# A two-layer hybrid transformer on one core: the end of the first layer's mixer, its second norm and its first feed-forward tiles, done by halves of the token columns

## What is computed

```
def modulate(x, g, shift, scale):
    return rms_norm(x, g) * (1 + scale) + shift
...
        acc = gates[..., 0, :] * (outs[0] @ w_branch[0])
...
        return acc @ w_out
...
def sq_relu_mlp(h, w1, w2):
    return jnp.square(jax.nn.relu(h @ w1)) @ w2
...
        x = x + g1 * o_lat
        x = x + g2 * sq_relu_mlp(modulate(x, norm2_g[l], sh2, sc2), w_ff1[l], w_ff2[l])
        if need_ctx:
            x_ctx = x_ctx + cg1 * o_ctx
            x_ctx = x_ctx + cg2 * sq_relu_mlp(modulate(x_ctx, norm2_g[l], csh2, csc2), w_ff1[l], w_ff2[l])
```

## Time and profile before

| | us |
|---|---|
| median of 3 runs | 1434.37 |
| the three runs | 1432.66, 1434.37, 1436.02 |
| the profiled execution | 1435.79 |
| its span in the trace | 1434.0 |
| PE busy in it | 1403.9 (98%) |
| DVE, ACT, POOL busy | 950.1 (66%), 656.4 (46%), 209.4 (15%) |
| mean granted clock of PE | 0.998 |

### The profile page before, as it was taken

The page is one execution under the profiler, slowest core; times in us unless marked ns, Lnnn a source line. Parts: engine busy times, 40 slices in busy tenths (PEclk is TensorE's granted clock), DMA queues, the critical chain, the costliest instruction groups (busy, mean ns, idle before and its releaser), DMA issues.

```text
span 1434.0 us, 24978 instructions
## 1 busy us (share of the span) xinstructions
PE 1403.9 (98%) x10474; PEld 1217.8 (85%) x10474; DVE 950.1 (66%) x1479; ACT 656.4 (46%) x969; POOL 209.4 (15%) x172
## 2 busy tenths in 40 slices
PE   8999999999999999999999999999999999999999
PEld 4889877786678888888888888889888779999999
DVE  6797467857446666699756655588387955775564
ACT  5722534364164444543224423553365645564462
POOL 0000001334111220131002200000013511121130
PEclk9999999999999999999999999999999999999999
DMA  9632323033153323266555665141343334556553
GB/s 383 233 110 75 112 101 133 30 100 110 42 193 128 130 84 146 97 217 247 199 204 190 211 217 177 49 142 61 106 153 129 125 126 148 176 206 206 191 194 116
DMA packets 37409, 215.07 MB, mean 150 GB/s; under 512 B 4017, under 2 KB 7729, under 8 KB 13617
## 3 DMA queue, kind: packets, MB, share of 16 engines
q1 hardware_dynamic: 37298, 213.48, 42.3%
HBM read 211.37 MB, written 2.10 MB: 149 GB/s over the span
## 4 chain that ended last, share of the span: by engine, by line
PE 87%; DVE 6%; ACT 3%; DMA 1%; issue 1%; POOL 0%; SPq 0%; DVEq 0%; ACTq 0%
PE ps L1234 11%; PE ps L1235 11%; PE ps L1236 11%; PE ps L608 9%; PE ps L609 9%; PE ps L610 9%; PE ps L833 3%; PE ps L585 2%; PE ps L620 2%; PE ps L622 1%; PE ps L621 1%; DVE parts L2052 1%; DVE arena L2433 1%; PE ps L730 1%; PE ps L1177 1%
## 5 line engine op out<-in xcount | busy, mean ns | idle before, releaser
L1236 PE MATMUL ps<-parts 128*128 128x512 f32 (+1 forms) x960 | 314.0, 327 | 0.0
L610 PE MATMUL ps<-parts 128*128 128x512 f32 (+1 forms) x944 | 313.6, 332 | 0.0
L1234 PE MATMUL ps<-parts 128*128 128x512 f32 (+1 forms) x928 | 303.6, 327 | 0.0
L1235 PE MATMUL ps<-parts 128*128 128x512 f32 (+1 forms) x928 | 303.6, 327 | 0.0
L1602 ACT ACTIVATE parts<-ring 128x1024 fp32r<-128x1024 f32 x124 | 124.4, 1051 | 221.8 <-PE ps L1236 186.7
L2094 DVE TENSOR_TENSOR parts<-ring,parts 128x1024 fp32r<-128x1024 f32 x124 | 150.9, 1258 | 112.1 <-ACT parts L1602 111.9
L1236 PEld LDWEIGHTS ps<-parts 128*128 128x128 f32 x960 | 182.9, 191 | 12.9
L610 PEld LDWEIGHTS ps<-parts 128*128 128x128 f32 x944 | 180.2, 191 | 13.9
L1234 PEld LDWEIGHTS ps<-parts 128*128 128x128 f32 x928 | 176.8, 191 | 12.6 <-DVE parts L2102 0.2
L1235 PEld LDWEIGHTS ps<-parts 128*128 128x128 f32 x928 | 176.8, 191 | 12.4
L608 PE MATMUL ps<-parts 128*128 128x512 f32 (+1 forms) x544 | 185.2, 340 | 1.0 <-ACT arena L1855 1.0
(11 more groups left out here) (323 smaller groups left out, 2478.8 us busy)
## 6 DMA issues: line engine op xcount, KB each, us to landing
ring<-in_w_ff SPq DMA_DIRECT2D x64, 1024.0 KB, 4.8
ring<-in_w_in SPq DMA_DIRECT2D x58, 1024.0 KB, 4.9
ring<-in_w_mod_rows SPq DMA_DIRECT2D x31, 1024.0 KB, 4.8
arena<-in_w_mod SPq DMA_DIRECT2D x8, 1024.0 KB, 17.4
arena<-in_w_mod_rows SPq DMA_DIRECT2D x8, 1024.0 KB, 10.7
ring<-in_w_branch SPq DMA_DIRECT2D x32, 256.0 KB, 5.2
ring<-in_w_out SPq DMA_DIRECT2D x8, 1024.0 KB, 4.9
ring<-in_w_in SPq DMA_DIRECT2D x6, 512.0 KB, 12.1
```

Source lines behind the costliest of these rows:

```text
L610: last = pe.matmul(ps[0:m, 0:n], w_lo[:, k, c], hi, start=False, stop=(k == KD - 1))
L1234: pe.matmul(ps[:, 0:nt], w_hi[:, k, c], hi, start=(k == 0), stop=False)
L1235: pe.matmul(ps[:, 0:nt], w_hi[:, k, c], lo, start=False, stop=False)
L1236: last = pe.matmul(ps[:, 0:nt], w_lo[:, k, c], hi, start=False, stop=(k == kt - 1))
```

## The change

Three things are done for the latents (half 0) first and for the context (half 1) after, in the first layer only:

- output tiles 6 and 7: PE makes 6 and 7 for the latents, then 6 and 7 for the context, each by 24 matmuls of 256 columns (`last_output_tiles`). The squares' sum of the latents stands between the context's tile 6 and tile 7.
- the second norm: squares, sum, root, norm and split by halves on ACT and DVE (two new `norm_halves`). The sum of the context stands on PE inside the feed-forward, behind feature tile 2 of the latents.
- the first four feed-forward tiles: all eight feature tiles for the latents, then all eight for the context (`ff_first_halves`).

The five products of `busy` fall away in the first layer. ACT's copy of feed-forward block 1 now stands behind the square of tile 5 and ahead of that of tile 6; DVE's subtraction stands ahead of the sum of square 5 and of the residual of tile 6. SP's list is the same. The second layer keeps its code.

```diff
@@ -745,6 +757,59 @@
...
+            def last_output_tiles(l):
+                w_hi, w_lo = split(l, ("out", 3))
+                for s in range(2):
+                    a = slice(s * LAT, (s + 1) * LAT)
+                    for m in (KD - 2, KD - 1):
+                        key = ("wo", l, m) if s else ("wo", l, m, "first")
+                        ps = bank(key)[:, 0:LAT]
+                        c = slice((m % 2) * P, (m % 2 + 1) * P)
+                        if s and m == KD - 1:
+                            half_sum(l, 1, 0)
+                        for k in range(KD):
+                            if s == 0 and m == KD - 2 and k % 4 == 0:
+                                pe.wait_ge(*s_ml.at(("w", l, ("out", 3), k // 4)))
+                            hi, lo = [in_turns(x[:, k, a]) for x in (A_HI, A_LO)]
+                            pe.matmul(ps, w_hi[:, k, c], hi, start=(k == 0), stop=False)
+                            pe.matmul(ps, w_hi[:, k, c], lo, start=False, stop=False)
+                            last = pe.matmul(ps, w_lo[:, k, c], hi, start=False, stop=(k == KD - 1))
+                        last.then_inc(*product.up(key))
+                new_last[("out", l, 3)] = ("wo", l, KD - 1)
+            def half_sum(l, w, s):
+                ps = bank(("ss", l, w, s), fixed=s)
+                a = slice(s * LAT, (s + 1) * LAT)
+                pe.wait_ge(*s_sum.at(("sum", l, w, KD - 2, s)))
+                pe.matmul(ps[:, 0:LAT], tab("ones"), ACC[:, 0, a], start=True, stop=False)
+                pe.wait_ge(*s_sq.at(("sq", l, w, KD - 1, s)))
+                pe.matmul(ps[:, 0:LAT], tab("ones"), ACC[:, KD - 1, a], start=False, stop=True)\
+                    .then_inc(*product.up(("ss", l, w, s)))
+            def ff_first_halves(l):
+                tiles = [(f, j, bank(ff_product(l, f, j))) for f in range(2) for j in range(2)]
+                for s in range(2):
+                    a = slice(s * LAT, (s + 1) * LAT)
+                    for k in range(KD):
+                        pe.wait_ge(*s_h.at(("h", l, 1, k, s)))
+                        for f, j, ps in tiles:
+                            w_hi, w_lo = [w.rearrange("p (k c) -> p k c", k=KD)[:, k, j * P:(j + 1) * P] for w in ff_parts(l, f)]
+                            if s == 0 and j == 0 and k % 4 == 0:
+                                pe.wait_ge(*s_wlo.at((l, f, k // 4)))
+                            pe.matmul(ps[:, a], w_hi, in_turns(H_HI[:, k, a]), start=(k == 0), stop=False)
+                            pe.matmul(ps[:, a], w_lo, in_turns(H_HI[:, k, a]), start=False, stop=False)
+                        pe.wait_ge(*s_hl.at(("hl", l, k, s)))
+                        for f, j, ps in tiles:
+                            w_hi = ff_parts(l, f)[0].rearrange("p (k c) -> p k c", k=KD)[:, k, j * P:(j + 1) * P]
+                            last = pe.matmul(ps[:, a], w_hi, in_turns(H_LO[:, k, a]), start=False, stop=(k == KD - 1))
+                            if s and k == KD - 1:
+                                last.then_inc(*product.up(ff_product(l, f, j)))
+                        if s == 0 and k == 2:
+                            half_sum(l, 1, 1)
...
@@ -1326,13 +1391,17 @@
                     mla_output(l, t)
                 gate(l, MLA, AHEAD[l] - 1)
                 merge(l, MLA, ahead=[(MLA, m) for m in range(AHEAD[l])])
-                for b in range(4):
+                for b in range(4 if l else 3):
                     for j in range(2):
                         parted(("wo", l, 2 * b + j), l, ("out", b), j, A_HI[:, :, inner(l)], A_LO[:, :, inner(l)], nt,
                                "a" if b + j == 0 else None)
                     new_last[("out", l, b)] = ("wo", l, 2 * b + 1)
-                norm_sum(l, 1)
-                ff_first(l)
+                if l == 0:
+                    last_output_tiles(l)
+                    ff_first_halves(l)
+                else:
+                    norm_sum(l, 1)
+                    ff_first(l)
                 for f in range(1, FF_STEPS):
                     if f > 1:
...
+            def root(l, w, s):
+                a = slice(s * LAT, (s + 1) * LAT)
+                ps = read(act, ("ss", l, w, s))
+                freed(("ss", l, w, s), "squares", ("ln", l, w, s))
+                act.activation(RS[:, 0, a], ps[:, 0:LAT], ACT.Ln, bias=tab("eps")).then_inc(*s_sq.up(("ln", l, w, s)))
+                act.wait_ge(*s_sq.at(("ln", l, w, s)))
+                act.activation(RS[:, 0, a], RS[:, 0, a], ACT.Exp, scale=-0.5).then_inc(*s_sq.up(("rt", l, w, s)))
...
+            def norm_halves(l):
+                def half_square(k, s):
+                    a = slice(s * LAT, (s + 1) * LAT)
+                    act.wait_ge(*s_x.at(("x" if s else "first", l, 0, k)))
+                    act.activation(ACC[:, k, a], X[:, k, a], ACT.Square, scale=D ** -0.5).then_inc(*s_sq.up(("sq", l, 1, k, s)))
+                def half_high(k, s):
+                    a = slice(s * LAT, (s + 1) * LAT)
+                    act.wait_ge(*s_nrm.at(("n", l, 1, k, s)))
+                    act.activation(H_HI[:, k, a], NR[:, k, a], ACT.Identity, bias=modv[:, l, 24 + k, s:s + 1])\
+                        .then_inc(*s_h.up(("h", l, 1, k, s)))
+                act.preload_act_table_set("natural_log_exp_and_others")
+                for k in range(KD - 2):
+                    if k in (0, 2, 4):
+                        part_high(l, ("out", 1 + k // 2))
+                    square(l, 1, k)
+                    if k in (4, 5):
+                        split_high(l, k - 4)
+                half_square(KD - 2, 0)
+                half_square(KD - 1, 0)
+                root(l, 1, 0)
+                half_square(KD - 2, 1)
+                half_high(0, 0)
+                half_high(1, 0)
+                half_square(KD - 1, 1)
+                for k in range(2, KD):
+                    half_high(k, 0)
+                    if k == 4:
+                        root(l, 1, 1)
+                for k in range(KD):
+                    half_high(k, 1)
...
@@ -1970,7 +2087,65 @@
...
+            def half_residual(l, m, s):
+                a = slice(s * LAT, (s + 1) * LAT)
+                key = ("wo", l, m) if s else ("wo", l, m, "first")
+                ps = read(dve, key)
+                freed(key, "residual", ("x" if s else "first", l, 0, m))
+                dve.scalar_tensor_tensor(out=by_halves(X[:, m, a]), in0=from_turns(ps[:, 0:LAT]), scalar=modv[:, l, 16 + m, s:s + 1],
+                                         in1=by_halves(XR[:, m, a]), op0=ALU.mult, op1=ALU.add)\
+                    .then_inc(*s_x.up(("x" if s else "first", l, 0, m)))
+            def half_sum(l, s):
+                a = slice(s * LAT, (s + 1) * LAT)
+                k = KD - 2
+                dve.wait_ge(*s_sq.at(("sq", l, 1, k, s)))
+                dve.wait_ge(*s_sum.at(("sum", l, 1, k - 1)))
+                dve.tensor_tensor(ACC[:, 0, a], ACC[:, 0, a], ACC[:, k, a], ALU.add).then_inc(*s_sum.up(("sum", l, 1, k, s)))
+            def norm_halves(l):
+                def half_norm(k, s):
+                    a = slice(s * LAT, (s + 1) * LAT)
+                    if k == 0:
+                        dve.wait_ge(*s_sq.at(("rt", l, 1, s)))
+                    dve.scalar_tensor_tensor(out=NR[:, k, a], in0=X[:, k, a], scalar=coefv[:, l, 1, k, s:s + 1], in1=RS[:, 0, a],
+                                             op0=ALU.mult, op1=ALU.mult).then_inc(*s_nrm.up(("n", l, 1, k, s)))
+                def half_low(k, s):
+                    a = slice(s * LAT, (s + 1) * LAT)
+                    dve.wait_ge(*s_h.at(("h", l, 1, k, s)))
+                    dve.scalar_tensor_tensor(out=H_LO[:, k, a], in0=NR[:, k, a], scalar=modv[:, l, 24 + k, s:s + 1],
+                                             in1=H_HI[:, k, a], op0=ALU.add, op1=ALU.subtract)\
+                        .then_inc(*s_hl.up(("hl", l, k, s)))
+                half_residual(l, KD - 2, 0)
+                half_sum(l, 0)
+                half_residual(l, KD - 1, 0)
+                half_residual(l, KD - 2, 1)
+                half_norm(0, 0)
+                half_sum(l, 1)
+                half_norm(1, 0)
+                half_residual(l, KD - 1, 1)
+                for k in range(2, KD):
+                    half_low(k - 2, 0)
+                    half_norm(k, 0)
+                half_low(KD - 2, 0)
+                half_low(KD - 1, 0)
+                half_norm(0, 1)
+                for k in range(1, KD):
+                    half_norm(k, 1)
+                    half_low(k - 1, 1)
+                half_low(KD - 1, 1)
...
@@ -2099,8 +2274,8 @@
                 nt = T if l == 0 else LAT
                 dve.wait_ge(*s_f1.at(("high", l, m)))
                 dve.wait_ge(*s_fp.at(("sq", l, m)))
-                dve.tensor_tensor(by_halves(HID_LO[:, m % 16, inner(l)]), from_turns(SG[:, m % 3, 0:nt]),
-                                  by_halves(HID_HI[:, m % 16, inner(l)]), ALU.subtract)\
```

(20 more changed lines are left out.)

3 lines of the change are left out of this document (added).

## The result

The changed kernel takes 1437.08 us, median of 20 runs (1434.26 to 1441.37), against 1433.28 for the kernel before, also 20 runs (1431.86 to 1437.34). The ratio is 1.0022, 95% interval 1.0015 to 1.0030: slower by 2 to 4 us. The forecast was 1436.8.

A forecast was written before the change was run, and what follows sets the result against it. PE was taken to bound the kernel (87% of the last chain). Terms -3.25 + 1.12 + 2.73 + 0.3, stepwise 0.8 us later, plus 1.6 half clock make 2.4: 1434.37 + 2.4 = 1436.8 us, range 1433.3 to 1438.6.

The forecast's parts named there:

- The number: Whole kernel: 1434.37 (median of three runs before) + 2.4 = 1436.8 us; chances 0.68 within 0.2%, 0.27 slower, 0.05 faster.
- The load: First layer's second norm: ACT's copy of block 1 waits about 3.2 us, to 559.4, holding the latent squares and residuals.
- The stall: PE at the sum of the latents: 2.4 us idle before the first product, 2.73 us lost in all.
- Halving: Splitting 144 matmuls of 512 columns into 256 columns at 0.1118 us each loses 1.12 us on PE.
- case C: Rival: the chain isn't held by the load; -3.25 + 1.12 + 0.3 = -1.8 us, 1432.5; chance 0.10.
- The low part of feature tile 0: First feed-forward tiles: DVE makes it only behind the context's residual of tile 7; PE stalls about 0.3 us.
- The clock: Behind the stall, from about 567: one stretch of PE at half clock, costing 1.6 us.
- the two longest idle stretches: PE idle 1.92 us (to 212.76) and 2.62 (to 1117.36), each followed by half clock; shorter ones of 1.23 to 1.58 weren't.
- B: Rival: the chain is held by the load but the clock stays; 1434.37 + 0.8 = 1435.2 us; chance 0.26.
- The sum: PE ends the four feed-forward tiles 0.8 us later, plus 1.6 for half clock: 2.4 us.
- The step that failed: After the four feed-forward tiles (590.64): PE has no wait until the second layer's norm, so the kernel's end moves equally.
- Case D: Rival: two stretches of half clock behind the stall, from tile 7 to feature tile 5; 4.2 us, 1438.5; chance 0.12.

The follow-up runs named there:

- e1: Changed kernel with ACT's copy of feed-forward block 1 back behind the latent squares, DVE's subtraction behind tile 7's latent residual; 1433.23 us, ratio 0.9996.
- e4: e1, and besides DVE makes the latent low part of feature tile 0 ahead of the context's residual of tile 7; 1432.82 us, ratio 0.9990.
- e2: Changed kernel with the five idle products put back on PE ahead of the sum of the latents; 1437.65 us, ratio 1.0023.
- c1: The kernel before, unchanged, measured against itself as a control; 1435.14 us against 1434.33, ratio 1.0002.
- e3: The kernel before without the five idle products of the first layer's second norm; 1436.78 us, ratio 1.0018.
- c2: The changed kernel measured again, against the kernel before; 1437.05 us, ratio 1.0021.
- e5: e4, and at the context's last feature tile PE finishes each of the four feed-forward tiles before the next; 1432.79 us, ratio 0.9988.
- e6: Changed kernel, and at the context's last feature tile PE finishes each of the four feed-forward tiles before the next; 1435.59 us, ratio 1.0011.
- c3: e1 measured again, against the kernel before; 1433.33 us, ratio 0.9987.
- c4: e4 measured again, against the kernel before; 1433.20 us, ratio 0.9988.

## Why the prediction held, point by point

- **The number.** That 1437.08 lies so near the forecast 1436.8 is partly luck. The base of the forecast, 1434.37 from three runs, was 1.1 above the 1433.28 of the twenty; the difference, forecast as 2.4, came out as 3.8 by medians and 3.2 by the ratio. The two errors nearly cancel. The ratio, 0.22% (0.15 to 0.30), lies on the bound between "within 0.2%" (chance 0.68) and slower (0.27). What held is the mechanism in the stretch, which the next points check.
- **The load.** Right, and it's the cause. Copy at 559.45 on the clock of before, measured 556.40 + 3.07 = 559.47. Latent residual of tile 6 at 563.4, measured 563.45. First sum product at 564.97, measured 564.98. e1 shows that undoing this alone takes 4.5 us off.
- **The stall.** 2.73 worked out as a whole. Measured, PE idles 2.26 before the sum. The two sum products start 0.75 apart where 0.43 is their pace, so about 0.3 lies there: 2.6.
- **Halving.** 0.1118 us for a matmul of 256 columns in the first layer too: tile 6 to tile 7 and the feed-forward tiles run at that pace, for all the other addresses. With nothing held, e1 gives 36.13 - 34.23 = 1.9, where case C said 1.8. With the 109.2 ns of the Trainium skill ("TensorE: Matmul & The Clock Gate", section "Back-to-back issue gap") it would have been 2.6, an estimate; no run here shows that pace.
- **The low part of feature tile 0.** 0.3 worked out, 0.24 measured, 0.35 won in e4.
- **The clock.** 1.6 worked out, 1.57 measured between the changed kernel and e2. Half clock began at 563.5, 1 to 2 us after the idle stretch. The argument from the two longest idle stretches was weaker than it looked, though: c1, the same code as before, has the same 2.62 us of idle, before 1114.59, and no half clock behind it (PE's timeline, and c1's table by stretch):

```profile
1114.59 1.60 PE L772 MATMUL ps<-tf,aroot 128*128 128x128 f32 x12 [2.62 <-DVE aroot L2530]
```

```profile
1112.00:1116.00 4.00, 1.41 (x12) 1.41 (x13) 3.12 (x6) 3.96 (x5) 2.19 (x3) 1.00 0.01 2
1116.00:1120.00 4.00, 4.00 (x19) 3.27 (x19) 3.98 (x4) 0.00 (x0) 3.92 (x3) 1.00 0.42 106
```

The changed kernel's first profile has none there either, after 2.52 us; the ten others do. And shorter idle stretches than the prediction allowed for had half clock behind them: 1.41 us near 180 in e3, c2 and e5, not in the nine others. So an idle stretch of either length brings half clock in some executions and not in others, and B deserved its chance. Both profiles of the changed kernel had half clock behind the stall, and e6's had too; whether its other runs had it always isn't shown. The mean clock of whole runs can't tell: it is 1.000 in 35 of 105 runs of before and in none of the 32 of the changed kernel, but also in only 2 of the 58 of e1, e4, c3, c4 and e5, which have no stall.
- **The sum.** 2.4 forecast, 2.57 measured in the stretch. The whole kernel is 2.7 to 3.8 above before by medians, depending on the group of runs, and 3.2 by pooled means.
- **The step that failed**, though the forecast as a whole held, is "from there PE has no wait until the second layer's norm; what is won or lost by 590.64 moves the end of the kernel by as much". PE had no wait there, but DVE behind it had almost no slack. With short matmuls at the end, the first hidden tile comes 3 x (0.2158 - 0.1118) = 0.31 us later against PE, DVE carries that through seven blocks, and PE waits in block 8. That makes 0.45 us more, 3.0 in all by the changed kernel's profiles. I costed the new order of the last feature tile at nothing without looking at who takes its products.
- **Case D** didn't come: no second stretch of half clock followed the stall, in either profile of the changed kernel.

The rest of the difference between stretch and time in the kernels with halves (e1 and e4 have 1.9 and 2.25 less in the stretch and gain 0.9 and 1.2 by pooled means, standard errors 0.4 and 0.3) is not all in block 8. The profiles show where more of it lies: the second layer's second norm, whose code is the same in all. PE idles 0.53 to 0.54 before its sum in before, c1, e2, e3 and e6, and 0.67 to 1.29 in the changed kernel, c2, e1, c3, e4, c4 and e5. One load makes the difference, that of the second layer's first feed-forward block. In the changed kernel (timeline of ACT and PE):

```profile
1248.79 2.01 ACT L1719 ACTIVATE parts<-ring 128x1024 fp32r<-128x1024 f32 x2 [0.35 <-DMA ring<-in_w_ff]
...
1254.42 0.67 PE L826 MATMUL ps<-ACC,tf 128*128 128x256 f32 x2 [1.01 <-DVE ACC L2214]
```

ACT copies that block 5.6 us before the sum and waits for it. The load takes 4.7 to 4.9 us from issue to landing in before, c1, e2 and e3, 5.6 in e6, and 5.7 to 6.3 in the seven others. From 5.7 on each tenth of it is a tenth of idle time: 5.71 in c4 gives 0.67, 6.04 in the changed kernel 1.01, 6.32 in c2 1.29. Half clock follows in five of the seven, and there PE needs 177.4 us from this sum to its last product, against 176.1 in the seven profiles without it: 1.3 us. It is the mechanism of the first layer once more, a copy that comes before its load has landed and holds what stands behind it, this time by some tenths.

Why the load is longer can be read off in part. In its first 3 us the DMA view of the changed kernel (issue of the load; queues from 1242.73 to 1245.73) has a packet of another queue, called instruction, of 16 KB:

```profile
ring<-in_w_ff SPq DMA_DIRECT2D x1, 1024.0 KB, 6.0
```

```profile
q8 instruction: 1, 0.02, 3.5%
```

In before, c1 and e3 that packet comes 4.0 to 4.4 us after the load's issue, in e2 0.06 before it, and in the eight others 0.9 to 2.0 after it. Over all twelve profiles, I took the 1 MB loads of output and feed-forward weights that had no other load beside them in their first 4.5 us. 345 of them had no such packet from 1 us before their issue to 3.8 after it, and took 4.56 to 5.17 us (median 4.79); 50 had one 0.5 to 3.2 us after their issue, and took 5.06 to 6.32 (median 5.56). The 28 with a packet at the edges between took 4.65 to 5.90. The two go together in the traces, but that one causes the other isn't shown: no kernel here moves such a packet alone. Two or four profiles of a kernel are also too few to say how much of the open 1 us it makes over all runs.

## What to carry to other kernels

When a step is moved ahead in an in-order list, ask first when its input is there, not only whether its output is wanted earlier: a copy that used to come 1.9 us after its load's landing came 3.2 before it, and everything behind it on two engines waited, 4.5 us in all with the half clock that followed. Fill a gap before taking away the products that keep PE busy in it, and look for the engine that has no slack where PE has no wait: there, splitting the last matmuls short makes their consumer late. And where whole runs vary by more than the change is worth, measure the stretch that the change touches: it repeated to 0.02 us, while the medians moved by 1. Then follow the trace behind the stretch as well: the waits in block 8 and in the second layer don't lie in it.

## What the runs showed of the hardware

- The same idle stretch of PE (2.62 us, same code) was followed by half clock in one execution of the kernel before and not in another; over all twelve profiles it is 2.52 to 2.62 us long and half clock followed in ten. An idle stretch of 1.41 us near 180 was followed by it in three of twelve. With 2.25 to 2.29 us idle before the sum it followed in all three profiles.
- With the same code, PE's wait near 212 was 1.92 us in one profile of the kernel before and absent in the other (c1): the load of 256 KB that ACT waits for ahead of it took 7.80 us from issue to landing in the first and 5.41 in the second.
- A stretch at half clock cost 1.57 us (changed kernel against e2) and 1.42 (e3 against before) in the middle of dense matmuls, and 1.3 behind the second layer's second norm.
- A load of 1 MB with no other load beside it in its first 4.5 us took 4.56 to 5.17 us in 345 cases without a packet of the instruction queue near its start, and 5.06 to 6.32 in 50 cases where such a packet of 16 KB came 0.5 to 3.2 us after its issue; the cause isn't shown. Where these packets fell differed between kernels: in e2 none of them fell into the second layer's first feed-forward load, and in the changed kernel one did.
